# Attention in a two-layer backbone: transposed tile in two halves, softmax sums from ones beside V, division of the value products on VectorE, value products one unit later

## What is computed

```python
def attention(q, k, v):          # 8 query heads, 2 key/value heads, 64 columns each
    ...
    s = jnp.einsum('bqhgd,bshd->bhgqs', qi, k).astype(jnp.float32)
    p = jax.nn.softmax(s, axis=-1).astype(v.dtype)
    return jnp.einsum('bhgqs,bshd->bqhgd', p, v)
```

## Time and profile before

| what | us |
|---|---|
| median of 3 runs | 2190.36 (2189.11 to 2195.18) |
| profiled execution, its own time | 2191.78 |
| span of its profile | 2190.0 |
| PE busy in it | 2124.9 |
| DVE busy in it | 1329.9 |
| ACT busy in it | 804.8 |

### The profile page before, as it was taken

One profiled execution on the slowest core, in us unless ns is written; L12 is line 12 of the kernel. 1 busy time (PEld: TensorE's weight loads), 2 busy tenths in 40 slices (PEclk: granted clock), 3 DMA queues, 4 the chain that ended last, 5 costly groups with the idle time before them and its releaser, 6 DMA issues.

```text
span 2190.0 us, 28107 instructions
## 1 busy us (share of the span) xinstructions
PE 2124.9 (97%) x11340; PEld 1789.5 (82%) x11340; DVE 1329.9 (61%) x1809; ACT 804.8 (37%) x1189; POOL 787.1 (36%) x366
## 2 busy tenths in 40 slices
PE   9999999999999999999999999899999999999997
PEld 7877888888888888888888887778777877888885
DVE  7369899855873688847616785989854362111113
ACT  5457411233224522222212356662244353222223
POOL 3310123232435433323323365004344475444442
PEclk8999999999999999999999999999999999999998
DMA  7100012132453234533323313002232423322321
GB/s 274 58 30 1 25 57 64 34 121 92 142 164 108 73 128 126 183 116 126 106 78 115 93 66 111 20 1 82 86 93 82 143 79 97 96 94 90 96 87 67
DMA packets 63200, 202.62 MB, mean 93 GB/s; under 512 B 7136, under 2 KB 8416, under 8 KB 63072
## 3 DMA queue, kind: packets, MB, share of 16 engines
q1 hardware_dynamic: 58608, 191.56, 27.0%
q10 hardware_dynamic: 4464, 9.28, 1.2%
HBM read 195.17 MB, written 5.64 MB: 92 GB/s over the span
## 4 chain that ended last, share of the span: by engine, by line
PE 80%; DVE 15%; ACT 3%; issue 1%; DMA 1%; POOL 1%; ACTq 0%; DVEq 0%; POOLq 0%
PE ps L560 73%; DVE conv_acc L1716 3%; DVE ps L1716 2%; DVE unit_stats L1677 2%; PE ps L586 1%; DVE pt1l L1697 1%; DVE pt0l L1697 1%; DVE probs L1691 1%; PE ps L795 1%; PE ps L629 1%; PE ps L647 1%; PE ps L638 1%; PE ps L816 1%; PE ps L668 1%; DMA w_raw<-in_w 1%
## 5 line engine op out<-in xcount | busy, mean ns | idle before, releaser
L455 POOL TENSOR_TENSOR w_l<-w_raw,w_h 128x1024 fp32r<-128x1024 f32 (+3 forms) x296 | 677.3, 2293 | 1283.0 <-ACT w_h L954 1282.9
L560 PE MATMUL ps<-h_h,w_h 128*128 128x512 f32 (+1 forms) x1296 | 428.0, 370 | 8.4 <-ACT t L1234 4.2
L560 PE MATMUL ps<-h_l,w_h 128*128 128x512 f32 (+1 forms) x1296 | 425.2, 368 | 0.0
L560 PE MATMUL ps<-h_h,w_l 128*128 128x512 f32 (+1 forms) x1296 | 424.7, 368 | 0.0
L954 ACT ACTIVATE w_h<-w_raw 128x1024 fp32r<-128x1024 f32 (+3 forms) x296 | 277.5, 939 | 236.0 <-PE ps L560 148.7
L560 PEld LDWEIGHTS ps<-h_h,w_h 128*128 128x128 f32 x1296 | 243.3, 188 | 59.0 <-ACT t L1234 6.0
L560 PEld LDWEIGHTS ps<-h_h,w_l 128*128 128x128 f32 x1296 | 244.4, 189 | 44.0
L560 PEld LDWEIGHTS ps<-h_l,w_h 128*128 128x128 f32 x1296 | 243.9, 188 | 42.6 <-issue 1.2
L1547 DVE CUSTOM_DVE_ANT_0 ps<-ada_raw,c_row 128x1024 f32<-128x1024 f32 x160 | 271.0, 1694 | 10.5 <-DMA ada_raw<-in_ada 5.4
L560 PE MATMUL ps<-f_h,w_h 128*128 128x258 f32 (+1 forms) x672 | 173.1, 339 | 0.9 <-DVE t L1902 0.9
L560 PE MATMUL ps<-f_h,w_l 128*128 128x258 f32 (+1 forms) x672 | 173.5, 340 | 0.0
(11 more groups left out here) (256 smaller groups left out, 3220.9 us busy)
## 6 DMA issues: line engine op xcount, KB each, us to landing
w_raw<-in_w SPq DMA_DIRECT2D x216, 512.0 KB, 3.6
ada_raw<-in_ada SPq DMA_DIRECT2D x80, 512.0 KB, 3.7
w_raw<-in_w SPq DMA_DIRECT2D x56, 256.0 KB, 3.2
w_raw<-in_w SPq DMA_DIRECT2D x16, 384.0 KB, 3.1
ada_near<-in_ada SPq DMA_DIRECT2D x10, 512.0 KB, 10.2
ada_far<-in_ada SPq DMA_DIRECT2D x6, 512.0 KB, 14.8
x_again<-in_x ACTq DMA_DIRECT2D x8, 384.0 KB, 7.5
x_between<-x SPq DMA_DIRECT2D x8, 384.0 KB, 2.9
```

Of the source, the lines that this page charges most:

```text
L455: nc.gpsimd.tensor_tensor(wl[:, s % RING, 0:n], raw[:, s % RAW, 0:n], wh[:, s % RING, 0:n], ALU.subtract).then_inc(split, 1)
L560: ins = nc.tensor.matmul(at(out, c0, c1), w[:, s % RING, b * P:(b + 1) * P], m[:, kt, first + c0:first + c1], start=(kt == 0 and n == 0), ...
```

## The change

The exponentials are no longer scaled before the transposes. V's high part lies in two tiles, one for each key/value head, with that head's 64 columns in the left half and 64 columns of ones in the right half; the second tile lies over `t2`, and the q1 tile uses `t3` in its place. A value product with the high part of V then has 128 output partitions: the upper 64 hold the row sums. DVE takes the reciprocal of those (64x256) and multiplies the lower 64 partitions by it into `o_raw`; ACT's copy into `o_raw` is gone, and so are the row sums by `accum_out`, and DVE's reciprocal and scaling of each unit. The transposed tile is handled in two halves, each in a PSUM bank of its own: two groups of three transposes (context: two), two high-part copies on ACT, two low-part subtractions on DVE, each with its own semaphore steps. A value product is scheduled one unit later, and PE's order in loop u becomes scores(u + 1), values, transposes(u - 1). ACT writes V's high part in two instructions and the ones in two more; DVE makes V's low part in two.

```diff
-                     "q1": (acc[:, 7], t1, t2), "q2": (acc[:, 4], acc[:, 5], acc[:, 6]),
+                     "q1": (acc[:, 7], t1, t3), "q2": (acc[:, 4], acc[:, 5], acc[:, 6]),
...
 def value_steps(us):
-            for u in range(2, len(us) + 2):
-                if us[u - 2][3] == us[u - 2][4] - 1:
-                    parts = 1 if us[u - 2][2] == CTX else 2
-                    todo += [(u - 2, part, parts) for part in range(parts)]
-                n = 1 if u < len(us) + 1 else len(todo)
+            for u in range(3, len(us) + 3):
+                if us[u - 3][3] == us[u - 3][4] - 1:
+                    parts = 1 if us[u - 3][2] == CTX else 2
+                    todo += [(u - 3, part, parts) for part in range(parts)]
+                n = 1 if u < len(us) + 2 else len(todo)
...
+        def turned(unit, half):
+            n = KT // 2 - 1 if q_tiles(unit) == 1 else CTX // P
+            return psf[:, 2048 + LAT * half:2048 + LAT * half + n * P]
...
# PE
                 def transposes(u):
-                    take("B", "pt", ly, u)
-                    pe.wait_ge(*seen("normed", ly, u))
-                    for k in range(nk * q_tiles(us[u]) // P):
-                        ins = nc.tensor.transpose(at(B, k * P, (k + 1) * P), pr[:, u % 2, k * P:(k + 1) * P], ident)
-                    ins.then_inc(*pe_done.up("pt", ly, u))
+                    pe.wait_ge(*seen("free", "scores", ly, u))
+                    n = turned(us[u], 0).shape[1]
+                    for half in range(2):
+                        take(("B", half), "pt", ly, u, half)
+                        for k in range(0, n, P):
+                            c = half * n + k
+                            ins = nc.tensor.transpose(turned(us[u], half)[:, k:k + P], pr[:, u % 2, c:c + P], ident)
+                        ins.then_inc(*pe_done.up("pt", ly, u, half))
...
                     for k in range(part * share, (part + 1) * share):
-                        for n, (v, p) in enumerate(((vh, ph), (vh, pl), (vl, ph))):
-                            ins = nc.tensor.matmul(ODs[b % 2][0:HD, 0:2 * P], v[:, k, d0:d0 + HD], p[:, k, :],
-                                                   start=(k == 0 and n == 0), stop=(k == nk // P - 1 and n == 2))
+                        out = ODs[b % 2][:, 0:2 * P]
+                        nc.tensor.matmul(out, vh[h // 4][:, k, :], ph[:, k, :], start=(k == 0), stop=False)
+                        nc.tensor.matmul(out[0:HD], vl[:, k, d0:d0 + HD], ph[:, k, :], start=False, stop=False)
+                        ins = nc.tensor.matmul(out, vh[h // 4][:, k, :], pl[:, k, :], start=False,
+                                               stop=(k == nk // P - 1))
...
# ACT, before the units
-                nc.scalar.activation(vh[:].rearrange("p a b -> p (a b)"), at(B, 0, T),
-                                     ACT.Copy).then_inc(*act_hi.up("vh", ly))
+                for g in range(KV):
+                    nc.scalar.activation(vh[g][:, :, 0:HD], group_columns(at(B, 0, T), g), ACT.Copy).then_inc(
+                        *(act_hi.up("vh", ly) if g else act_hi.up()))
+                for g in range(KV):
+                    ins = nc.scalar.activation(vh[g][:, :, HD:P], ones[:, 0:1].to_broadcast([P, 6, HD]), ACT.Copy)
+                    ins.then_inc(*(act_hi.up("ones", ly) if g else act_hi.up()))
...
# DVE, in loop u
-                        link(v.reciprocal(ust[:, 3, c:c + n], ust[:, 2, c:c + n]), dve_tmp)
-                        for r in range(n):
-                            p_r = pr[:, (u - 1) % 2, r * nk:(r + 1) * nk]
-                            v.tensor_scalar(p_r, p_r, ust[:, 3, c + r:c + r + 1], None, ALU.mult).then_inc(
...
+                        for half in range(2):
+                            dve.wait_ge(*seen("pth", ly, u - 2, half))
+                            v.tensor_tensor(key_rows(pl, us[u - 2], half), by_key(turned(us[u - 2], half)),
+                                            key_rows(ph, us[u - 2], half), ALU.subtract).then_inc(
+                                *dve_lo.up("free", "pt", ly, u - 2, half))
+                    for done, part, parts in plan.get(u - 1, ()):
+                        if part == parts - 1:
+                            h, q0, nk, q, nq, b = us[done]
+                            dve.wait_ge(*seen("pv", ly, b))
+                            o, inverse = ODs[b % 2], t1[0:HD, 2 * P * (b % 2):2 * P * (b % 2 + 1)]
+                            link(v.reciprocal(inverse, o[HD:P, 0:2 * P]), dve_tmp)
+                            p = HD * (h % 2)
+                            v.tensor_tensor(o_raw[p:p + HD, h // 2, q0:q0 + 2 * P], o[0:HD, 0:2 * P], inverse,
+                                            ALU.mult).then_inc(*dve_out.up("free", "pv", ly, b))
```

More of the change, by code:

```diff
@@ L211, in build @@
         ada_raw = sb("ada_raw", [2, KT * P])
-        t1, t2, t3 = (sb(n, [800]) for n in ("t1", "t2", "t3"))
+        t2, vh_second = overlay("region_t2", 4 * 800, [("t2", [800], F32)], [("v_second", [6, P], F32R)])
+        t1, t3 = sb("t1", [800]), sb("t3", [800])
+        vh = (vh_first, vh_second)
         const = sb("const", [NC])
@@ L358, in q_scale, with key_rows, by_key, group_columns @@
             return token_rs[:, c:c + HEADS * (q_tiles(unit) - 1) + 1:HEADS]
[L360 to L366, removed]
-            h, q0, nk, q, nq, b = unit
-            n = q_tiles(unit) * P
-            out = ap[:, 0:nk // P, q * n:(q + 1) * n]
-            return out if n == P else out.rearrange("p k (r q) -> p k r q", q=P)
+        def turned(unit, half):
+            n = KT // 2 - 1 if q_tiles(unit) == 1 else CTX // P
+            return psf[:, 2048 + LAT * half:2048 + LAT * half + n * P]
+        def key_rows(ap, unit, half):
+            h, q0, nk, q, nq, b = unit
+            if q_tiles(unit) == 2:
+                return ap[:, 0:CTX // P, half * P:(half + 1) * P]
+            return ap[:, 3 * half:3 * half + 3, q * P:(q + 1) * P]
+        def by_key(ap):
+            return ap.rearrange("p (k q) -> p k q", q=P)
+        def group_columns(ap, g):
+            return ap.rearrange("p (k c) -> p k c", c=P)[:, :, HD * g:HD * (g + 1)]
         pool_last, pool_adds = (0, 2, 4, 6), (4, 5, 6, 7)
@@ L808, in values @@
                             pe.wait_ge(*seen("tile", ly, "v"))
-                        pe.wait_ge(*seen("free", "pt", ly, u))
+                            pe.wait_ge(*seen("ones", ly))
+                    pe.wait_ge(*seen("free", "pt", ly, u, part if parts == 2 else 1))
                     ph, pl = pt(b)
@@ L823, in _ @@
                 plan = value_steps(us)
-                for u in range(len(us) + 2):
+                for u in range(len(us) + 3):
                     if u + 1 < len(us):
                         scores(u + 1)
+                    for step in plan.get(u, ()):
+                        values(*step)
                     if 1 <= u <= len(us):
                         transposes(u - 1)
-                    for step in plan.get(u, ()):
-                        values(*step)
                 for j in range(1, BR):
@@ L1147, in _ @@
                     act.wait_ge(x_stored, 16 * KT)
[L1149 to L1153, removed]
-                plan = value_steps(us)
-                for u in range(len(us) + 3):
+                for u in range(len(us) + 1):
                     if u < len(us):
@@ L1644, in _ @@
                 dve.wait_ge(*seen("vh", ly))
-                v.tensor_tensor(vl[:].rearrange("p a b -> p (a b)"), at(B, 0, T),
-                                vh[:].rearrange("p a b -> p (a b)"), ALU.subtract).then_inc(
-                    *dve_lo.up("free", "vt", ly))
+                for g in range(KV):
+                    ins = v.tensor_tensor(vl[:, :, HD * g:HD * (g + 1)], group_columns(at(B, 0, T), g),
+                                          vh[g][:, :, 0:HD], ALU.subtract)
+                    ins.then_inc(*(dve_lo.up("free", "vt", ly) if g else dve_lo.up()))
                 noted[("tile", ly, "v")] = noted[("free", "vt", ly)]
@@ L1671, in _ @@
                 us = units(ly)
-                for u in range(len(us) + 2):
+                plan = value_steps(us)
+                for u in range(len(us) + 5):
                     if u < len(us):
```

41 lines of the change are left out of this document (14 added, 27 removed).

## The result

The changed kernel takes 2215.72 us (median of 4 runs, 2213.0 to 2218.56) against 2189.74 us of the kernel before (4 runs, 2186.26 to 2195.18): a ratio of 1.0121, 95% interval 1.0097 to 1.0146. It is 26 us slower. I had said 13 us slower (2203.4), with a range of 2193 to 2220. The result lies in that range, but above the forecast's own bounds (2197 to 2213), and it is twice the difference that I had summed.

The account below looks back on a forecast made before the run. DVE's list was taken to set the pace, with a 2.77 us loop in layer 1; +9.2 us in layer 0, +2.2 in layer 1 and +1.6 of waits made +13.0, so 2203.4 us; range 2193 to 2220.

Parts of the forecast that it names:

- What bounds the kernel now: Attention: DVE without idle sets layer 0's pace, 13.57 us a head; a 2.77 us transposes-copy-subtraction loop sets layer 1's.
- The price of the reciprocal: DVE, each value product: a 64x256 reciprocal takes 1.74 us, at 6.2 ns for each further column, 40 times.
- third rival: DVE's wide reciprocal is dearer: 8.3 ns a column, 2.3 us each, +22 us, 2225 us in all; chance 4%.
- The cost of a product around its reciprocal: DVE, each product: 0.03 us wait, then a multiplication of 0.42 less 0.09 overlap; 2.10 us with the reciprocal.
- After the stretch, layer 1: After layer 1's attention: DVE's output work starts 2 us later, all taken up by its 5.4 us wait for PE.
- Both ends of a stretch: Attention's start and end: pipe fill 1.5 and 2.3 us, first copies 0.2, last values 0.7 and 2.1, two divisions -4.2.
- the 1.6 that I had put in for waits of DVE: Both attentions: DVE still waits 0.1 us in each of 16 heads, +1.6 us.
- second rival: Attention: PE's clock falls once a head, 3 to 4 us at half speed, losing 1 to 1.7; 2219 to 2230; 11%.
- V's split and the ones: Before the attention units: three more instructions on ACT and one on DVE, counted 0, at most 2 us a layer.
- ACT's relief: Attention: ACT loses the accumulator reading and the copy to `o_raw`; with 5 us of 20 to spare, worth nothing by itself.

Follow-up runs that it names:

- halves alone: The kernel before with only the transposed tile handled in two halves, each in its own bank; 2180.19 against 2188.58 us, ratio 0.9958.
- ones alone: The changed kernel with the transposed tile in one piece again, the rest of the change kept; 2237.6 against 2189.13 us, ratio 1.0220.
- low part later: The changed kernel with layer 1's low part of the attention output made after the second convolution input; 2213.1 against 2190.31 us, ratio 1.0098.

## Why the prediction came out as it did

The sign and its cause were right; the size was half of what came. That the result lies in the range is owed to the range's margin, not to the sum.

**What bounds the kernel now**: right. DVE's list set the pace in layer 0, and the loop through B in layer 1 is cut by the halves (2.77 to 2.72 us). What I had not seen is how much the waits cost outside the mean head: the halves alone earn 8 us.

**The price of the reciprocal**, the term that decided the sign: right to about 1% (1.74 forecast, 1.759 measured), and shown as the cause by two experiments that change it alone. My third rival (8.3 ns a column) is out, and with it the reading of the Trainium skill's repeat count as cycles a column ("VectorE: DVE Perf Modes", section "Walkthrough: the 8-slice pipeline in each mode"): 6.25 ns it is.

**The cost of a product around its reciprocal**: mis-sized, by a wrong reading. I let every DVE instruction overlap its neighbour by 0.09 us, "since the overlap is seen between all neighbours there". It is not: in the earlier trace rows the 128x1 reciprocal of 180.79 has ended by 180.94, and the scaling starts at 180.98. In the changed kernel the wide reciprocal starts when the pair of low parts has ended (1424.93 to 1425.94, then 1425.98), and the multiplication is often followed without overlap. That belongs to the place and not to the operation: a copy put there starts as late (165.79), and the 128x1 reciprocal of the halves alone starts at 1403.17, before the record ahead of it (1403.10, 0.16) has ended. It makes 0.19 us for each product: (16.33 - 15.75)/3 = 0.19 and (12.57 - 12.20)/2 = 0.19. Over 40 products that is 7.7 us.

**After the stretch, layer 1**: failed. "In layer 1 DVE waits 5.4 us for PE, which takes up all": those waits lie behind the place where PE needs DVE, the second convolution input. PE comes there after three GEMMs, 16.9 us; DVE had been ready 0.95 us sooner, and that was all the cover. The low part then started 1.3 us later, and it took 2.2 us longer because POOL's subtraction ran beside it, a term that the prediction does not have. PE's 2.7 us of waiting and 1.7 us of clock behind them make 4.4 of the 4.6 us lost; the move of the low part gave back 4.3. In layer 0 the cover held, since three GEMMs are 25.3 us there and DVE had read its second input after 23.2: the group from 258.30 is as long as in the earlier trace rows.

**Both ends of a stretch** came out 0.8 us in layer 0 and 0.9 in layer 1 longer than forecast, beyond the divisions. Together: 7.7 + 1.7 + 4.6 = 14.0, less the 1.6 that I had put in for waits of DVE, is 12.4, against the 13.0 that I was short; the difference is within what runs of one kernel differ by.

**The clock**, my second rival: it did not come once a head. PE is idle nearly a quarter of the time in the changed kernel's mid-stretch by the profile's count, and more in the ones alone (14.63 busy of 20), and the granted clock is 1.00 in all of layer 0's attention and in layer 1's from 1399 to 1487 us. The Trainium skill ("TensorE: Matmul & The Clock Gate", section "HAM oscillation — how this bites in real kernels") did not promise it either: the waits between bursts in its example are 3 to 5 us, those in the changed kernel's attentions 1.8 us at most, and I had read "just this" into it. Yet the clock was not out of the matter. It is at 0.50 at the start of layer 1's attention (1395 to 1399, where the pipeline fills), at its end (1487 to 1491, right after a wait of 1.83 us), and after the wait of 2.7 us. And it can fall in mid-stretch: in the low part later, whose layer 0 attention is the same code, it is at 0.50 from 212 to 215 us. That head took 16.51 us for 16.30, so in this one case a fall cost 0.2 us and not the 1 to 1.7 of my rival; this fits my own argument against it, that a slower PE first eats its own idle time.

**V's split and the ones** at nothing: not tried alone, and no wait before the two attentions is longer for them. **ACT's relief** is worth nothing by itself, as said: it idles 9.3 of 20 us now.

## What to carry to other kernels

Price a removed operation and its replacement by columns on the engine that sets the pace: a 128x1 reciprocal is nearly free, and broadcasting sums first and inverting 256 columns of copies costs eleven times as much, more than the scaling it saves. Cut the loop and share the scaling with an idle engine instead, and give PE work to do meanwhile; an order that is worth nothing behind one bound can be worth 8 us when the bound moves. A backlog at the end of a stage is covered only by waits that lie before the next place where the other engine needs its result; and what a later start runs into there (a subtraction on POOL, here) can cost more than the delay.

## What the runs showed of the hardware

- A reciprocal on DVE takes 0.16 us and 6.25 ns a column (64x128 959 ns, 64x256 1759 ns), six times the 1.04 ns of other operations.
- Some neighbouring DVE instructions overlap in their records by 0.09 us, others not at all. The 64x256 reciprocal and the 64x256 copy in its place both start 0.02 to 0.04 us after the end of the pair ahead; a 128x1 reciprocal started 0.09 us before the end of its neighbour.
- A DVE subtraction or copy within SBUF takes longer beside POOL's subtraction of 128x1024: four 128x512 subtractions 4.70 us (changed kernel) against 2.50 (before), a 128x512 copy 2.57 (before) against 0.43 (low part later).
- POOL scales 128x768 in 2.20 us and 128x384 in 1.47 us while DVE works, against 0.62 and 0.42 on DVE.
- With PE busy 15.19 or 14.63 of 20 us by the profile's count, its granted clock was 1.00 in these stretches. It fell to 0.50 after a wait of 1.83 us (1486.47) and after one of 2.67 (1513.32), each time for 3 to 4 us.
